# Replicating the decay rows over the partitions: eight transfers through DRAM, or eight matmuls into a PSUM bank

## The reference, cut to what matters

```python
a_cs  = cumsum(dt * a)                       # per head, along the tokens
seg   = a_cs[l] - a_cs[s]
decay = exp(where(l >= s, seg, -inf))
y[l]  = sum_s  (C[l] . B[s]) * decay[l, s] * dt[s] * x[s]   (+ d_skip * x[l])
```

## Time and profile before

| | |
|---|---|
| median of 3 runs | 1858.37 us (1856.11 to 1860.89) |
| the profiled execution | 1858.37 us, of which the span is 1856.6 us |
| PE busy | 1799.0 us, 97% of the span, 13052 matmuls |
| DVE, ACT, POOL busy | 1138.6, 897.7 and 153.3 us (61%, 48%, 8%) |
| DMA | 326.46 MB, mean 176 GB/s |

### The profile page before, as it was taken

The page is one execution under the profiler, slowest core; times in us unless marked ns, Lnnn a source line. Parts: engine busy times, 40 slices in busy tenths (PEclk is TensorE's granted clock), DMA queues, the critical chain, the costliest instruction groups (busy, mean ns, idle before and its releaser), DMA issues. The chain is left out here.

```text
span 1856.6 us, 35122 instructions
## 1 busy us (share of the span) xinstructions
PE 1799.0 (97%) x13052; PEld 1676.2 (90%) x13052; DVE 1138.6 (61%) x1790; ACT 897.7 (48%) x1350; POOL 153.3 (8%) x189
## 2 busy tenths in 40 slices
PE   6999999999999899999999998999999999999998
PEld 5899998899888778999999788999999999988886
DVE  6555655656666666766555556676666666644445
ACT  6465454554445455454444445545444554433333
POOL 1001110000101100000000000100000000033331
PEclk9999999999999999999999999999999999999999
DMA  7555555565444455666565464666666656665554
GB/s 234 166 148 152 159 160 174 182 182 171 137 137 141 132 182 172 177 184 181 170 172 173 160 194 145 188 199 194 198 196 192 191 183 192 202 199 193 194 192 139
DMA packets 235612, 326.46 MB, mean 176 GB/s; under 512 B 12432, under 2 KB 170420, under 8 KB 234896
## 3 DMA queue, kind: packets, MB, share of 16 engines
q1 hardware_dynamic: 233440, 318.61, 55.6%
q0 software_dynamic: 1808, 6.69, 1.2%
q10 hardware_dynamic: 288, 0.11, 0.0%
HBM read 323.24 MB, written 2.13 MB: 175 GB/s over the span
## 5 line engine op out<-in xcount | busy, mean ns | idle before, releaser
L1658 DVE TENSOR_TENSOR w_low<-raw,w_high 128x1024 fp32r<-128x1024 f32 x603 | 736.4, 1230 | 616.7 <-ACT w_high L1162 615.1
L1162 ACT CAST w_high<-raw 128x1024 fp32r<-128x1024 f32 x603 | 626.8, 1049 | 657.4 <-PE bank L509 339.0
L507 PE MATMUL bank<-hT_high,w_high 128*128 128x256 f32 x2640 | 739.1, 280 | 8.1 <-DVE hT_low L1675 2.8
L508 PE MATMUL bank<-hT_low,w_high 128*128 128x256 f32 x2640 | 732.8, 278 | 0.0
L509 PE MATMUL bank<-hT_high,w_low 128*128 128x256 f32 x2640 | 732.7, 278 | 0.0
L507 PEld LDWEIGHTS bank<-hT_high,w_high 128*128 128x128 f32 x2640 | 497.6, 188 | 15.4 <-issue 6.2
L508 PEld LDWEIGHTS bank<-hT_low,w_high 128*128 128x128 f32 x2640 | 497.2, 188 | 0.1
L509 PEld LDWEIGHTS bank<-hT_high,w_low 128*128 128x128 f32 x2640 | 497.3, 188 | 0.0
L515 PE MATMUL bank<-w_high,yT_high 128*128 128x512 f32 x384 | 153.5, 400 | 3.8 <-issue 2.0
L517 PE MATMUL bank<-w_high,yT_low 128*128 128x512 f32 x384 | 150.8, 393 | 0.0
L516 PE MATMUL bank<-w_low,yT_high 128*128 128x512 f32 x384 | 150.8, 393 | 0.0
(11 more groups left out here) (320 smaller groups left out, 2128.1 us busy)
## 6 DMA issues: line engine op xcount, KB each, us to landing
raw<-in_w_up SPq DMA_DIRECT2D x176, 512.0 KB, 4.5
raw<-in_w_in SPq DMA_DIRECT2D x88, 512.0 KB, 3.7
raw<-in_w_down SPq DMA_DIRECT2D x88, 512.0 KB, 4.5
raw<-in_w_swa SPq DMA_DIRECT2D x72, 512.0 KB, 3.7
raw<-in_w_c SPq DMA_DIRECT2D x50, 512.0 KB, 3.8
raw<-in_w_mlao SPq DMA_DIRECT2D x32, 512.0 KB, 3.8
raw<-in_w_swao SPq DMA_DIRECT2D x32, 512.0 KB, 3.9
raw<-in_w_out SPq DMA_DIRECT2D x32, 512.0 KB, 3.7
```

The costliest lines, as they stand in the source:

```text
L507: nc.tensor.matmul(to, h, act_h[:, chunk, :], start=first, stop=False, skip_group_check=True)
L508: nc.tensor.matmul(to, h, act_l[:, chunk, :], start=False, stop=False, skip_group_check=True)
L1162: nc.scalar.copy(whi(tile, i, n), raw[s][:, :]).then_inc(high_made, 1)
L1658: v.tensor_tensor(wlo(tile, i, n), raw[s][:, :], whi(tile, i, n).bitcast(F32), ALU.subtract).then_inc(low_made, 1)
```

## The change: what it does

The copy of `acs` in DRAM, its store and the eight transfers of `spread_decays` are gone. In their place DVE's `select(u)` writes, for each of two heads, `acs` times a column of the identity, which leaves the one row of that head and zeros in the other 15 (`sel`, 16x2x256, in the place where `decay_rows` was). PE's `ssm_bcast(i, u)` multiplies a 16x128 matrix of ones with `sel`, 16x512, in float32, into bank 0, so that both heads' rows stand on all 128 partitions. DVE's `segments(u)` reads them from bank 0. `ssm_bcast(i, 0)` stands between tiles 7 and 8, `ssm_bcast(i, 1)` directly behind `ssm_mix(i, 0)`. The first tile of the next step, which also writes bank 0, now waits for `segments(1)` too. On POOL, the three copies of `split_rows` that stood among the transfers become a loop.

```diff
-        decay_rows = gate[:, 0:2, :]
-        decays = nc.dram_tensor("decays_by_head_dram", (SSM_H, SEQ), F32, kind="Internal").ap()
+        sel = gate[0:SSM_H, 0:2, :]
...
+            def ssm_bcast(i, u):
+
+                n = i * 2 + u
+                after(pe, mb["q_out"], i + 1)
+                pe.wait_ge(sm["sel"], n + 1)
+                wait(pe, sm["seg"], n)
+                f32mm(banks[0], one16[:, 0:P], sel[:, :, :]).then_inc(sm["bcast"], 1)
...
-                            if k == 1:
-                                wait(pe, sm["y_out"], i * 2)
+                            if k < 2:
+                                wait(pe, sm[("seg", "y_out")[k]], i * 2)
...
                     tiles(6, 7)
                     if first:
                         pe.wait_ge(sm["dt_x"], 1)
+                    ssm_bcast(i, 0)
                     tiles(8, 9, 10)
                     ssm_mix(i, 0)
+                    ssm_bcast(i, 1)
...
+                def select(u):
+
+                    if project:
+                        for h in range(2):
+                            head = 2 * i + (8 * u + h)
+                            one = cst[0:SSM_H, head:head + 1] if isinstance(i, int) else cst[0:SSM_H, bass.ds(head, 1)]
+                            last = v.tensor_scalar(sel[:, h, :], acs[:, :], one, None, ALU.mult)
+                        last.then_inc(sm["sel"], 1)
...
-                        dve.wait_ge(sm["bcast"], n * 16 + 16)
+                        dve.wait_ge(sm["bcast"], n + 1)
...
-                                last = v.tensor_scalar(dec[:, h, at:at + nq], decay_rows[:, h, SEQ - nq:SEQ],
+                                last = v.tensor_scalar(dec[:, h, at:at + nq], banks[0][:, (h + 1) * SEQ - nq:(h + 1) * SEQ],
...
+                select(0)
                 tile(6)
...
                 segments(0)
+                select(1)
                 tile(9)
...
-            pool.wait_ge(sm["acs"], 1)
-            pool.dma_start(decays, acs).then_inc(sm["acs_out"], 16)
...
-            def spread_decays(n):
-
-                first = 2 * (n // 2) + 8 * (n % 2)
-                pool.dma_start(decay_rows, bass.AP(decays.tensor, first * SEQ, [[0, P], [1, 2 * SEQ]])).then_inc(sm["bcast"], 16)
-
-            pool.wait_ge(sm["acs_out"], 16)
-            spread_decays(0)
-            for i in range(4):
-                if i:
-                    split_rows(mb, i - 1, 2, 2 * (i - 1))
-                for u in range(2):
-                    n = 2 * i + u + 1
-                    if n < 8:
-                        pool.wait_ge(sm["seg"], n)
-                        spread_decays(n)
+            with pool.Fori(0, 3) as p:
+                chain.enter(p, 1)
+                split_rows(mb, p, 2, p * 2)
+            chain.leave(3)
```

More of the change, by code:

```diff
@@ L394, in program @@
         sm = names("ssm", "xr", "conv_in", "conv", "tanh", "xbc", "cb_done", "dt_exp", "dt_ln", "dt_x", "acs", "cols", "rb_cleared", "xs_psum",
-                   "xs_out", "cb_psum", "acs_out", "bcast", "seg", "exp", "m_ready", "y_psum", "y_out",
+                   "xs_out", "cb_psum", "sel", "bcast", "seg", "exp", "m_ready", "y_psum", "y_out",
                    "gated", "ss", "rstd", "yn", "y_tr", "y_high", "y_low")
```

## The result

The changed kernel takes 1871.01 us in the median of six runs (1866.25 to 1874.73). The kernel before takes 1858.92 us, also in six. The ratio is 1.0063, with a 95% interval of 1.0047 to 1.0081: 0.6% slower, which is 11.7 us by the ratio and 12.1 between the medians. The scatter goes with the mean granted clock of an execution: the fastest of the six has 0.997, the slowest 0.991. The forecast was +6.7 us with a range up to 1869.5, so the sign was right, the size was not, and the time lies just above the range. The profiled execution took 1870.36 us, 12.0 more than the one before.

A forecast was written before the change was run, and what follows sets the result against it. The prediction took PE, busy for 97% of the span, to bound the kernel. Products of 7.3 us less 0.6 given back in step 0 made +6.7 us on 1858.37, so 1865.1 us, with a range of 1861.0 to 1869.5.

The forecast's parts named there:

- What bounds the kernel: In this stage PE sets the end: a microsecond of work added to PE adds a microsecond to the kernel.
- Waits, DVE, removed transfers in steps 1 to 3: PE never waits for `sel` or bank 0; DVE gains about 8 us off the path; removed transfers are worth nothing.
- The product: Eight float32 products of 16x128 by 16x512 on PE: 4 x 0.96 + 4 x 0.86 = 7.3 us.
- the narrow contraction does not help as far as rows show: For PE's products: few partitions make them no cheaper, since a 33-partition product also scales to 0.86 us at 512 columns.
- 0.1 for four products and none for the others: Switch cost on PE: 0.1 us for a product between tiles 7 and 8, none directly behind `ssm_mix`.
- My bound of 1.06 a product: Upper bound for PE's products: 0.86 us plus 0.20 of transition each, 8.5 us for eight.
- The slow spacing: About 28 of the stage's 64 tiles start matmuls 0.118 us apart instead of 0.113; put at 0 in the sum.
- the term without a price: Tiles changing matmul spacing either way in the stage: from 3.1 us gained to 3.9 lost, 0 in the sum.
- tiles flip to the slow spacing: Rival: the new products make all the stage's tiles slow, the whole 3.9 us, time 1869; chance 0.06.
- The transfers in step 0: Without the first 256 KB of decays a weight tile lands sooner: 0.6 us given back, bounds 0 and 0.8.
- Held within 0.3%: Rival: PE's products cost only 0.46 us each, less 0.6, time 1861.5; cheap product chance 0.08.
- The transfers held PE back: Rival: slow spacing and step 0 idling come from the decay traffic, 5.7 us together; time 1856.4, chance 0.03.

The follow-up runs named there:

- full height: The changed kernel with the broadcast products made over all 128 partitions, zeros below row 16; 1866.07 us against 1859.71 for the kernel before, ratio 1.0032.
- products of 16 rows: The kernel before plus eight unread float32 products of 16x128 by 16x512, its transfers and readers kept; 1871.15 us.
- of 64 rows: The kernel before plus eight unread float32 products of 64x128 by 64x512; 1870.79 us.
- in fp32r: The kernel before plus eight unread fp32r products of 128x128 by 128x512; 1861.40 us.
- product ahead of `ssm_mix`: The changed kernel with each step's second product moved from behind `ssm_mix(i, 0)` to ahead of it; 1870.54 us.
- `select` twice: The changed kernel with DVE's `select` done twice for each pair; 1866.53 us.
- the one with the dip of the clock: The changed kernel with each 16-row product issued twice in a row; 1882.73 us.
- the kernel with the first of them later: The kernel before with the first decay transfer and the bias gather issued only after ACT cast the stage's ninth weight tile; 1858.48 us against 1858.95, ratio 1.0001.

## Why the prediction was wrong in size

**What bounds the kernel** was right. PE never idles in steps 1 to 3 of either kernel, and what the change adds to it is added to the time: 11.8 us in the stage, 12.0 in the profiled executions. From step to step of the loop PE takes 54.65 us after and 51.6 before, +3.05 where +1.8 was forecast.

**Waits, DVE, removed transfers in steps 1 to 3** were right. No wait of PE on `sel` or `dec` came up, and DVE's work grew by 7.4 us against 8 forecast. The DVE timeline after answers to the earlier trace rows:

```profile
891.43 1.38 DVE L2208 TENSOR_SCALAR constants<-bank,dt_and_decay_cols 128x256 f32<-128x256 f32 x4
892.73 0.60 DVE L2192 TENSOR_SCALAR gate<-gate,constants 16x256 f32<-16x256 f32 x2
...
894.83 1.40 DVE L2219 SCALAR_TENSOR_TENSOR constants<-constants,dt_and_decay_cols,cb_masked 128x256 f32<-128x256 f32 x4
```

`segments` takes 1.38 (1.3 forecast from the copy of 384 columns), `select` 0.60 (0.65). decay_products(0) ends at 896.23 and PE comes to `ssm_mix` at 897.95: 1.7 us of slack are left, where I had 1.4.

**The product is the step that failed.** Its core, 0.86 us for 512 float32 columns, was right: the product at full height costs just that, and so does a second narrow one. What failed is "the narrow contraction does not help as far as rows show", which asked only whether few rows make a product cheaper, and not whether they make it dearer., with 33 partitions, held the answer. There the product's end came 0.20 later than its two records say, and I read this as a switch between float32 and fp32r, which the scores and `ssm_mix`, both of full height, had shown to be nearly free. The line ahead of it in the same timeline shows a second loss:

```profile
804.17 0.28 PE L509 MATMUL bank<-hT_high,w_low 128*128 128x256 f32 x1
804.38 0.81 PE L542 MATMUL bank<-constants,rel_bias 33*8 33x384 f32 x2
```

From start to start this is 0.21 us and not 0.12. Put together, these rows point to the height. (That the loss behind is 0.20 there and 0.30 here is not explained; the product of the earlier trace rows has 8 stationary columns and not 128.) I took 0.1 for four products and none for the others. Measured are 0.30 for all eight, and 0.10 ahead of four. My bound of 1.06 a product was too low for the same reason: the columns were scaled, 0.20 taken as it stood, and the record ahead not looked at. This is 9.9 us (with `ssm_mix`) where I had 7.3, 2.6 too little.

**The slow spacing** was the term without a price, and the rival "tiles flip to the slow spacing" came in. With 36 tiles to flip I had priced it at 3.9; 20 flipped, for 2.1 us. I put 0 in the sum and gave it 0.06. That products of 16 or 64 rows bring them on is shown (42 to 48 slow tiles in the six kernels that have them, 31 at full height, 25 with fp32r, 26 without products), and that the weights' place changes the spacing. Why the same place has two spacings, and how a narrow product brings on the slower, stays open: the narrow products also hold the stream up for longer, and no run separates the two.

**The transfers in step 0** were given 0.6 us. In the profiled pair 0.3 came back: the timelines of ACT and PE after, which answer to the earlier trace rows, are

```profile
825.51 1.05 ACT L1171 CAST w_high<-raw 128x1024 fp32r<-128x1024 f32 x1 [3.20 <-DMA raw<-in_w_in]
...
827.77 0.23 PE L970 MATMUL bank<-constants,gate 16*128 16x16 f32 x1 [0.28 <-ACT gain_rows L1520]
```

ACT still waits 3.20 us for the tile (3.42 before), and PE 0.28. But one pair can't tell 0.3 from 0.6. From PE's start behind its wait for `w_low` to the start of the stage, the kernels with all eight decay transfers and the weights at float 16 take 12.31 (before), 13.06, 12.80 and 12.62 us (with products of 16 rows, of 64 rows and in fp32r), and those without the transfers 11.99 (after), 11.83 (product ahead of `ssm_mix`), 11.74 (`select` twice) and 12.37 us (full height); the one with the dip of the clock is left out. The means are 12.7 and 12.0. In two of the four without the transfers PE doesn't wait for the copies at all, though the bias gather is where it was. So 0.6 was a fair price, and the 0.3 of the pair lies within the scatter of this wait.

In sum: 2.6 for the borders and 2.1 for the slow tiles are the 4.7 us that the prediction lacked. With the 0.3 that this pair did not give back they make 5.0, which leads from +6.7 to +11.7; the profiled executions differ by 12.0, and the rest is rounding and scatter.

**The other rivals.** "Held within 0.3%" needed a record at 0.23; only fp32r has that. The Trainium skill ("TensorE: Matmul & The Clock Gate", section "Back-to-back issue gap") has 131 ns for a matmul of 512 columns in a stream, and the fp32r ones here cost 240 ns. "The transfers held PE back" is refuted by the same stage and the same slow tiles with the eight transfers and without them (199.92 and 199.91), and by the kernel with the first of them later: 0.58 us, and no slow tile fewer.

## What to carry to other kernels

On a kernel that PE bounds, taking away a DMA that nobody waits for gives nothing back (here in steps 1 to 3), and a matmul that replaces it costs all of its time. Don't price a small matmul by its columns alone: read in the trace the start of the matmul ahead of it and of the second one behind it, for a shape of the same height, and where it stands in a stream of full-height matmuls, try to fill it up to 128 rows with zeros (here 0.86 us instead of 1.16 to 1.26). Don't settle a wait of some tenths of a us by one pair of executions. Before a stream that bounds a kernel is blamed on traffic or the clock, try where its operands lie.

## What the runs showed of the hardware

- A float32 product of 512 columns costs 0.86 us at full height. With 16 or 64 rows among matmuls of full height it costs 1.16, and up to 0.10 more ahead of it. A second one right behind costs 0.85. PEld shows it: the next weight load waits 0.76 us, where at full height the next two wait 0.24 each.
- An fp32r matmul of 512 columns of full height costs 0.24 us, 3.6 times less than the float32 product.
- fp32r matmuls of 256 columns follow each other at 0.113 or 0.118 us with the weight tiles at float 16 of the slot, at 0.1165 to 0.120 at floats 8 and 24, and at 0.120 at floats 0 and 32, with the granted clock at its upper level, 2.4 GHz, throughout. Against float 16 that made the stage up to 6.1 us longer. At float 16 the same tiles of the same program can take either spacing.
- Behind one and the same wait of 2.00 us PE's granted clock fell to 0.50 in one execution and stayed at 1.00 in the others looked at.
